# A transposed copy of the input, partial first chunks and a reordered half-step schedule at the head of a two-layer trunk kernel

## The reference, cut to what matters

```python
def rms_norm(x, g):
    y = x * lax.rsqrt(jnp.mean(x * x, axis=-1, keepdims=True) + EPS)
    return y * g
def moba_mixer(h, w_qkv, q_gain, k_gain, w_o, pos):
    q, k, v = jnp.split(h @ w_qkv, 3, axis=-1)
    q = rope(rms_norm(q.reshape(B, S, A_HEADS, A_HEAD_DIM), q_gain), pos)
    k = rope(rms_norm(k.reshape(B, S, A_HEADS, A_HEAD_DIM), k_gain), pos)
    o = moba_attention(...)          # causal softmax(q k^T / sqrt(128)) v
    return o.reshape(B, S, D_MODEL) @ w_o
def reference(...):
    for i in range(DEPTH):
        h = rms_norm(x, norm_mix_g[i])
        x = x + (moba_mixer(h, ...) if i == 0 else retention_mixer(h, ...))
        x = x + sqrelu_mlp(rms_norm(x, norm_mlp_g[i]), mlp_w1[i], mlp_w2[i])
```

## Time and profile before

| | |
|---|---|
| median of 3 runs | 688.73 us (688.31 to 689.94) |
| the profiled execution, its own time | 689.67 us |
| span of its instructions | 687.8 us |
| PE busy | 664.2 us, 97% of the span |
| DVE, ACT, POOL busy | 420.4, 328.6, 27.8 us |
| moved by DMA | 121.93 MB, mean 177 GB/s |

### The profile page before, as it was taken

How to read it: one execution, slowest core, us unless ns; L and a number is a source line. 1 busy time by engine, 2 the same in 40 slices (tenths; PEclk the granted TensorE clock), 3 DMA queues, 4 the chain that set the end, 5 groups by cost and what they waited for, 6 DMA issues and landing times.

```text
span 687.8 us, 8852 instructions
## 1 busy us (share of the span) xinstructions
PE 664.2 (97%) x3293; PEld 558.7 (81%) x3293; DVE 420.4 (61%) x454; ACT 328.6 (48%) x423; POOL 27.8 (4%) x39
## 2 busy tenths in 40 slices
PE   2989899999999999999999999999999999999998
PEld 2868777888888888888888888888888888888886
DVE  2885755677777535446985456555468777743430
ACT  3765655475555433436444554553365555533320
POOL 3032200000000000000000000000000000000000
PEclk9999999999999999999999999999999999999999
DMA  8964344756655555563655554455646665555600
GB/s 286 336 217 149 122 123 123 229 152 204 195 183 183 186 200 203 187 202 124 190 193 180 180 176 130 177 182 154 202 133 199 194 205 195 185 183 186 211 1 30
DMA packets 81469, 121.93 MB, mean 177 GB/s; under 512 B 2032, under 2 KB 43152, under 8 KB 81440
## 3 DMA queue, kind: packets, MB, share of 16 engines
q1 hardware_dynamic: 80736, 119.55, 53.4%
q0 software_dynamic: 496, 1.90, 1.0%
q10 hardware_dynamic: 208, 0.08, 0.1%
HBM read 120.47 MB, written 1.05 MB: 177 GB/s over the span
## 4 chain that ended last, share of the span: by engine, by line
PE 83%; issue 5%; ACT 4%; DVE 4%; DMA 2%; POOL 1%; SPq 0%; DVEq 0%; ACTq 0%; POOLq 0%
PE acc L467 22%; PE acc L427 16%; PE acc L429 16%; PE acc L428 15%; PE acc L470 11%; ACT hi L658 2%; DVE lo L874 2%; DMA x<-in_x 2%; POOL small L383 1%; PE scr L483 1%; ACT probs L726 1%; DVE h_both L883 1%; PE scr L603 1%; POOL rot L403 1%; PE scr L615 1%
## 5 line engine op out<-in xcount | busy, mean ns | idle before, releaser
L874 DVE TENSOR_TENSOR lo<-raw,hi 128x2048 fp32r<-128x2048 f32 x112 | 256.8, 2293 | 141.2 <-ACT hi L658 141.2
L658 ACT ACTIVATE hi<-raw 128x2048 fp32r<-128x2048 f32 x112 | 214.6, 1918 | 127.8 <-PE acc L429 127.8
L467 PE MATMUL acc<-h_both,hi 128*128 128x512 f32 x640 | 223.1, 395 | 0.0
L470 PE MATMUL acc<-h_both,lo 128*128 128x256 f32 x640 | 177.8, 278 | 0.0
L467 PEld LDWEIGHTS acc<-h_both,hi 128*128 128x128 f32 x640 | 120.1, 188 | 28.2
L470 PEld LDWEIGHTS acc<-h_both,lo 128*128 128x128 f32 x640 | 120.3, 188 | 0.0
L427 PE MATMUL acc<-hi,aT_hi 128*128 128x512 f32 x256 | 99.7, 389 | 0.0
L429 PE MATMUL acc<-hi,aT_lo 128*128 128x512 f32 x256 | 99.6, 389 | 0.0
L428 PE MATMUL acc<-lo,aT_hi 128*128 128x512 f32 x256 | 99.6, 389 | 0.0
L427 PE MATMUL acc<-hi,h_both 128*128 128x512 f32 x224 | 91.3, 408 | 0.0
L429 PE MATMUL acc<-hi,h_both 128*128 128x512 f32 x224 | 88.4, 395 | 0.0
(11 more groups left out here) (114 smaller groups left out, 528.5 us busy)
## 6 DMA issues: line engine op xcount, KB each, us to landing
raw<-in_mlp_w SPq DMA_DIRECT2D x64, 1024.0 KB, 5.4
raw<-in_r_w_in SPq DMA_DIRECT2D x24, 1024.0 KB, 5.1
raw<-in_a_w_qkv SPq DMA_DIRECT2D x12, 1024.0 KB, 6.2
raw<-in_r_w_out SPq DMA_DIRECT2D x8, 1024.0 KB, 5.0
raw<-in_a_w_o SPq DMA_DIRECT2D x4, 1024.0 KB, 5.1
x<-in_x SPq DMA_DIRECT2D x2, 512.0 KB, 11.8
out_x<-x SPq DMA_DIRECT2D x4, 256.0 KB, 3.9
decay_sb<-in_decay POOLq DMA_DIRECT2D x1, 768.0 KB, 7.2
```

What stands on the lines that cost most here:

```text
L467: nc.tensor.matmul(bank, feat_view(hi, s)[:, kt, o * P:(o + 1) * P], h_both[:, kt, :, :].rearrange("p b t -> p (b t)"), start=kt == 0, sto ...
L470: m = nc.tensor.matmul(bank[:, 0:SEQ], feat_view(lo, s)[:, kt, o * P:(o + 1) * P], hT_hi[:, kt, :], start=False, stop=kt == KD - 1)
L658: nc.scalar.activation(hi[:, s, :], raw[:, s, :], ACT.Copy).then_inc(hi_ready, 1)
L874: nc.vector.tensor_tensor(lo[:, s, :], raw[:, s, :], hi[:, s, :].bitcast(F32), ALU.subtract).then_inc(lo_ready, 1)
```

## The change

1. **Input.** The host lays out x transposed as well (`xT_src`, two halves of 4 column blocks) and the identity with all norm gains in one array (`consts`). ACT and DVE make `h_both` straight from the loaded `xT_in`. The transposes of the gains and of x in norm 0 are gone. PE does four float32 matmuls on zeros instead, before its first product.
2. **Queues.** All in SP's queue, in this order: first half of xT, chunk 0 in four parts of 256 KB, second half of xT, chunks 1 and 2 in four parts each, `rope_t`, two gains, chunks 3 and 4, x whole (1 MB), chunk 5, `mask`, chunks 6 on. `rope_r_sb` is issued later, beside `decay_sb`. POOL issues nothing at the head.
3. **Parts.** For chunks 0 to 2 ACT and DVE make the high and low part in four pieces of 512 columns, and PE waits for each piece alone. The order on both: xT blocks 0 to 3, chunk 0, xT blocks 4 to 7, chunk 1, chunk 2.
4. **Squares of x.** ACT's squares and the row factor (`square`, `factors`) go to half step 7. var p is not before half step 8. A new step `left` (only the semaphore that frees the accumulator) stays where var was. Each p has its own sums (`head_sums`).
5. **Low parts.** ACT's high part stays at half step k (`high`), DVE's low part goes to k + 1 (`low`), for chunks 3 to 16.

```diff
 def attention_schedule():
     at = [[] for _ in range(SLOTS)]
     for k in range(0, SLOTS, 2):
-        at[k].append(("split", k // 2 + AHEAD))
+        at[k].append(("high", k // 2 + AHEAD))
+        at[k + 1].append(("low", k // 2 + AHEAD))
     for b in range(4):
         for t in range(TT):
             p = 2 * b + t
             at[4 * b + 3 + t] += [("rope", p), ("raw", p)]
-            at[4 * b + 4 + t].append(("var", p))
+            at[4 * b + 4 + t].append(("left", p))
+            at[max(4 * b + 4 + t, FACTORS_AT + 1)].append(("var", p))
...
+    first_to_last = ["O", "N", "v", "rope", "high", "low", "raw", "left", "square", "factors", "var", "T", "A",
+                     "P", "S", "E"]
     for k in range(SLOTS):
...
+FACTORS_AT = 7
...
+SQUARES_BEFORE = sum(what == "raw" for k in range(FACTORS_AT + 1) for what, _ in SCHEDULE[k])
+PARTS = 3
...
-            for n in range(2):
-                sp.dma_start(x[:, :, n * NC:(n + 1) * NC],
-                             xv[:, :, n * NC:(n + 1) * NC]).then_inc(x_in_ready[n], 16)
-            for c in range(1, 12):
+            def load_xT(n):
+                sp.dma_start(xT_in[:, 4 * n:4 * n + 4, :], xT_src[n]).then_inc(xT_in_ready[n], 16)
+
+            def load_parts(c):
+                for kt in range(4):
+                    sp.dma_start(tok_view(raw, c)[:, kt, :],
+                                 qkv_w[QKV_ORDER[c // 2], c % 2][:, kt, :]).then_inc(part_in[c][kt], 16)
+
+            load_xT(0)
+            load_parts(0)
+            load_xT(1)
+            load_parts(1)
+            load_parts(2)
+            sp.dma_start(rope_t[:], rope_a).then_inc(tables_in, 16)
+            for i, g in enumerate((a_q_gain, a_k_gain)):
+                sp.dma_start(gains[:, i, :], g.broadcast_to([P, P])).then_inc(tables_in, 16)
+            load_qkv(3)
+            load_qkv(4)
+            sp.dma_start(x[:], xv).then_inc(x_in_ready, 16)
+            load_qkv(5)
+            sp.dma_start(mask[:], causal).then_inc(mask_in, 16)
...
         def _(pool):
-            pool.dma_start(rope_t[:], rope_a).then_inc(tables_in, 16)
-            for i, g in enumerate((a_q_gain, a_k_gain)):
-                pool.dma_start(gains[:, i, :], g.broadcast_to([P, P])).then_inc(tables_in, 16)
-            pool.dma_start(mask[:], causal).then_inc(tables_in, 16)
-            pool.dma_start(rope_r_sb[:], rope_r).then_inc(tables_r_in, 16)
             half_set = pl.mark(nc.gpsimd.memset(half[:], -0.5))
             pool.wait_ge(pl.sem, half_set)
-            pool.wait_ge(tables_in, 16 * 4)
...
-            norm_power()
             pool.wait_ge(pl.sem, pl.now())
             pool.sem_inc(tables_g_ready, 1)
+            norm_power()
             for p_i in range(8):
...
+            pool.dma_start(rope_r_sb[:], rope_r).then_inc(tables_r_in, 16)
...
-                chunk_in(c_g, s)
+                parts = isinstance(c_g, int) and c_g == 0 and s < PARTS
+                if not parts:
+                    chunk_in(c_g, s)
...
                     for kt in range(4):
                         k = k0 + kt
+                        if parts and t == 0:
+                            if s < 2:
+                                pe.wait_ge(hT_ready, 4 + k + 1)
+                            if kt < 3:
+                                pe.wait_ge(part_lo_ready, 3 * s + kt + 1)
+                            else:
+                                chunk_in(c_g, s)
...
-            pe.wait_ge(ident_in_sem, 16)
-            pe.wait_ge(gains_in, 32)
-            nc.tensor.transpose(acc[:, 0, 0:4 * KD], gain_rows[:],
-                                ident[0:4 * KD, 0:4 * KD]).then_inc(gainsT_ready, 1)
-            for n in range(2):
-                pe.wait_ge(x_in_ready[n], 16)
-                transpose_x(0, range(4 * n, 4 * n + 4))
+            pe.wait_ge(zeros_ready, 1)
+            for _ in range(4):
+                nc.tensor.matmul(acc[:, 3, 0:SEQ], sT[:, 0:P], sT[:, 0:SEQ], start=True, stop=True)
+            pe.wait_ge(consts_in, 16)
...
+                if norm == 0:
+                    act.wait_ge(x_in_ready, 16)
+                    act.wait_ge(squares_qk, 4 * SQUARES_BEFORE)
...
-            act.dma_start(ident[:], ident_in).then_inc(ident_in_sem, 16)
-            for i, g in enumerate((norm_mix_g, norm_mlp_g)):
-                act.dma_start(gain_rows[i * 2 * KD:(i + 1) * 2 * KD, :],
-                              g.rearrange("l (kt p) -> (l kt) p", p=P)).then_inc(gains_in, 16)
-            act.wait_ge(gainsT_ready, 1)
-            nc.scalar.copy(gcol[:].rearrange("p a b -> p (a b)"), acc[:, 0, 0:4 * KD]).then_inc(gcol_ready, 1)
-            split(0, 0)
-            act.wait_ge(gcol_ready, 1)
-            norm_hi(0, range(KD))
-            split(0, 1)
-            norm_squares(0)
-            split(0, 2)
+            def first_hi(kts):
+                for kt in kts:
+                    act.wait_ge(xT_in_ready[kt // 4], 16)
+                    nc.scalar.activation(hT_hi[:, kt, :], xT_in[:, kt, :], ACT.Copy,
+                                         scale=gcol[:, GAIN[0], kt:kt + 1]).then_inc(hT_hi_ready, 1)
+
+            def part_hi(c):
+                for kt in range(4):
+                    act.wait_ge(part_in[c][kt], 16)
+                    nc.scalar.activation(tok_view(hi, c)[:, kt, :], tok_view(raw, c)[:, kt, :], ACT.Copy
+                                         ).then_inc(part_hi_ready if kt < 3 else hi_ready, 1)
+
+            act.dma_start(consts[:], consts_src).then_inc(consts_in, 16)
+            act.wait_ge(consts_in, 16)
+            first_hi(range(4))
+            part_hi(0)
+            first_hi(range(4, KD))
+            part_hi(1)
+            part_hi(2)
...
                 j, t = p_i // 2, p_i % 2
                 act.wait_ge(rope_read, p_i + 1)
-                if p_i == 0:
+                if p_i >= 1:
+                    act.wait_ge(squares_qk, 4 * p_i)
+                if p_i == SQUARES_BEFORE:
                     act.wait_ge(ssq_ready, 4)
-                else:
-                    act.wait_ge(squares_qk, 4 * p_i)
-                if p_i >= 2:
-                    act.wait_ge(pow_ready, p_i)
                 for h in range(4):
                     nc.scalar.activation(junk[:, h * P:(h + 1) * P], acc[:, p_i % 4, h * P:(h + 1) * P],
-                                         ACT.Square, accum_out=small[:, 4 * t + h:4 * t + h + 1]
+                                         ACT.Square, accum_out=head_sums[:, p_i, h:h + 1]
...
+            def first_lo(kts):
+                dve.wait_ge(consts_in, 16)
+                for kt in kts:
+                    dve.wait_ge(hT_hi_ready, kt + 1)
+                    nc.vector.scalar_tensor_tensor(hT_lo[:, kt, :], xT_in[:, kt, :],
+                                                   gcol[:, GAIN[0], kt:kt + 1],
+                                                   hT_hi[:, kt, :].bitcast(F32), ALU.mult,
+                                                   ALU.subtract).then_inc(hT_ready, 1)
+
+            def part_lo(c):
+                for kt in range(4):
+                    if kt < 3:
+                        dve.wait_ge(part_hi_ready, 3 * c + kt + 1)
+                    else:
+                        dve.wait_ge(hi_ready, c + 1)
+                    nc.vector.tensor_tensor(tok_view(lo, c)[:, kt, :], tok_view(raw, c)[:, kt, :],
+                                            tok_view(hi, c)[:, kt, :].bitcast(F32), ALU.subtract
+                                            ).then_inc(part_lo_ready if kt < 3 else lo_ready, 1)
+
+            def first_factors():
+                norm_factors(0)
+                own(nc.vector.tensor_scalar(nrm[:, 5, :], nrm[:, 0, :], EPS, None, ALU.mult))
+                own(nc.vector.tensor_scalar(nrm[:, 6, :], nrm[:, 0, :], EPS * P, None, ALU.mult))
+
+            nc.vector.memset(sT[:], 0.0).then_inc(zeros_ready, 1)
+            first_lo(range(4))
+            part_lo(0)
+            first_lo(range(4, KD))
+            part_lo(1)
+            part_lo(2)
...
                 j, t = p_i // 2, p_i % 2
@@ -928,6 +986,8 @@
                     dve.wait_ge(tok0_ready, j + 1)
                 else:
                     dve.wait_ge(used, 2 * j + 2 + RING)
+                if p_i == 0:
+                    dve.wait_ge(tables_g_ready, 1)
...
                 rr = rot[:, t, :].rearrange("p (h o d) -> p h o d", o=2, d=64)
                 nc.vector.tensor_tensor(rr, rr, ur, ALU.add).then_inc(rot_sum_ready, 1)
+            def head_left(p_i):
+                dve.wait_ge(squares_qk, 4 * p_i + 4)
+                dve.sem_inc(acc_free, 1)
+
             def head_variance(p_i):
                 j, t = p_i // 2, p_i % 2
-                ss = small[:, 4 * t:4 * t + 4]
+                ss = head_sums[:, p_i, :]
                 dve.wait_ge(squares_qk, 4 * p_i + 4)
-                dve.sem_inc(acc_free, 1)
                 if j % 2 == 0:
                     i = nc.vector.tensor_scalar(ss, ss, nrm[:, 6, t:t + 1], None, ALU.add)
```

(23 more changed lines are left out.)

70 lines of the change are left out of this document (35 added, 35 removed).

## The result

| | before | after |
|---|---|---|
| median | 688.55 us (687.75 to 689.94, 6 runs) | 693.0 us (691.32 to 695.07, 6 runs) |
| the profiled execution, its own time | 689.67 us | 693.57 us |
| span of its instructions | 687.8 us | 691.8 us |

The ratio is 1.0059, 95% interval 1.0045 to 1.0073: the change makes the kernel slower by 0.45 to 0.73%. The forecast was 680.9 (677.0 to 685.0), faster. It was off by 12 us, and in the sign.

The account below looks back on a forecast made before the run. PE, busy 97% of the span, was taken as the bound, improvable only in its gaps and slower stretches. Gains of 5.5 (T 2), 1.0 (T 6) and 1.3 (later low parts) sum to 7.8 us: median 680.9, range 677.0 to 685.0.

Parts of the forecast that it names:

- The step that failed: Behind the attention: largest sum of PE's waits for one line is 0.5 us, code left alone, so no gain or loss.
- Rival 4: Slower: gains in the weights' queue delay chunk 3; at 26.3 the 7.8 us are gone, at 30 us 692.4; chance 0.04.
- T 2: PE's transposes of the first k block, opened by DVE and POOL: at 46.5 in place of 52.01, gain 5.5 us.
- The first product: PE's first product in the head: at 7.5 instead of 16.87, 9.4 us earlier.
- Chunk 3: Weights landing in SP's queue: 17.5 without a slow stretch, 19.5 with it, 18.5 taken; ACT's high part then starts the chain.
- the term of 5.7 MB: Bytes loaded up to chunk 3 (xT, chunks 0 to 2, tables, chunk 3), at 0.393 MB per us.
- The POOL term: Before T 2: POOL's powers 1 and 2 and the scaling wait for DVE's low 7, ending at 43.4, and finish at 46.4.
- the 49 that the prediction named as a sign of being wrong: The prediction called itself wrong if T 2 opens before 44 or after 49.
- The clock: Behind the wait at T 2 the clock drops as before: no difference counted, bounds 0 and 1 us more.
- T 6: Later in the attention, PE waits 1.8 us for POOL's scaling: gain between 0 and 1.8, 1.0 taken.
- The later low parts: Low 13 and 14 move behind S 4 and S 6, easing 1.8 us of oT_lo waits: gain 1.3 us taken.
- rival 2: In the attention, later half steps give nothing; only T 2 moves, by 4.4 to 5.5 us: 683.2 to 684.4; chance 0.20.

Follow-up runs that it names:

- experiment 1: The changed kernel with an unused 384-byte tile in front of the arena, back at its old address: 686.56 us, ratio 0.9967 to before.
- experiment 2: The kernel before with gain_rows moved behind the arena and 128 bytes ahead of it, so the arena starts 384 bytes lower: 694.7 us, ratio 1.0095.
- experiment 7: experiment 1 with the two gains laid out for all partitions in memory, no row read 128 times: 684.24 us, ratio 0.9949 to before.
- experiment 10: experiment 1 with ten matmuls on zeros into an unused bank in front of T 2: 684.71 us, ratio 0.9960 to before.
- experiment 11: The changes of experiment 7 and experiment 9 together: 680.89 us, ratio 0.9891 to before.
- experiment 3: The changed kernel with 256 bytes of padding in front of the arena: 694.8 us.
- experiment 4: The changed kernel with weights, h_both and arena all moved, by paddings of 128 bytes in all: 685.27 us.
- experiment 9: experiment 1 with the squares of x and the row factor at half step 5 instead of 7: 683.37 us, ratio 0.9934 to before.
- experiment 5: The changed kernel with 128 bytes of padding in front of the arena: 684.65 us.
- experiment 6: The changed kernel with 448 bytes of padding in front of the arena: 691.87 us.
- experiment 8: experiment 1 with the low parts back in the half step of their high parts: 692.75 us, ratio 1.0076 to before.
- experiment 12: experiment 11 with the low parts from half step 20 on back in the half step of their high parts: 681.54 us, ratio 0.9895.

## Why the prediction was wrong, by its own steps

**The step that failed** is the sentence "Behind the attention the largest sum for one line is 0.5 us, and the change leaves that code alone". The code was left alone, its data were not: two small tiles changed in size, the arena moved by 384 bytes, and about 1,056 products got 5.7 ns longer. The prediction has no term for it. It is +6.0 us by the steps, +5.8 between the marks, +6.4 by experiment 1, +6.5 by experiment 2. With it, the sign of the result is explained: experiment 1 is the change without it, and is 2.0 us faster than before. That was shown both ways, by taking the shift out of after and by putting it into before. None of the four rivals had it. Rival 4, the one on the other side, had the right sign for a wrong reason: chunk 3 came at 20.9, far from the 26.3 at which it decides. That its 692.4 is near the 693.0 measured is luck.

**Experiment 1 against the sum of 7.8 us.** Experiment 1 lies 5.7 us above the forecast even so, and above its range. In the traces T 2 gained 2.4 us there in place of 5.5, and what was to gain 2.3 more behind T 2 gained nothing.

- *The first product*, forecast 7.5, came at 9.07. The sum had no term for ACT's table load of 1.28 us in front of the first block. PE waited 3.5 us for the first piece of chunk 0, and came to T 2 at 43.4, not at 39.9. As the forecast said, it made no difference to T 2.
- *Chunk 3*, forecast 18.5 between bounds of 17.5 and 19.5, was split from 20.94 on, beyond the slow bound. The reading that the gains cause the slow stretch was right (experiment 7), and so was its price: 2.2 us by the windows, 2.0 in the sum. ACT was not late, it stood idle 5.41 us for the load. What was too small is the term of 5.7 MB: added up from the windows, 6.4 MB had been moved when chunk 3's high part could start in after, and 6.3 MB at 18.85 in experiment 7. The 0.6 to 0.7 MB more can only be bytes of loads issued behind chunk 3, and at 0.393 MB per us they are 1.6 us. So chunk 3 without the stretch comes at 18.85, not at 17.5.
- *T 2*, forecast 46.5 (45.5 to 47.6), came at 48.77. The 2.3 us are chunk 3's 2.4. From chunk 3's high part to T 2 it was 28.0 us forecast and 27.8 measured: the order on DVE, the stand for the row factor (forecast "2 to 3 us", found 1.29 and 0.81), and the power held behind low 7 all stood as worked out. The POOL term, "43.4 + 0.9 + 1.0 + 1.05", was 45.76 to 48.72, 2.96 against 2.95. This term gave 3.2 in place of 5.5. In experiment 1, with chunk 3 at 21.69, T 2 is at 49.59, behind the 49 that the prediction named as a sign of being wrong.
- *The clock*, counted as no difference with a bound of 1. Its lower level lasted 6.8 us. The traces price it by the stretch from T 2 to x in kernels with the new schedule: 71.4 and 71.5 us without the lower level (experiments 10 and 11), 73.0 to 73.1 with 3.4 us of it (3, 4, 9), 73.4 to 74.3 with 6.8 (after, 1, 5, 6, 7). So the second 3.4 us, which before doesn't have, cost 0.3 to 1.3 us, 0.9 in the mean, near the forecast's bound.
- *T 6*, forecast a gain of 1.0: 1.8 of waits became 0.8 (6.2 less 5.4). Right.
- *The later low parts*, forecast 1.3: they gained nothing. In place of 1.8 us for `oT_lo` and 0.2 for `v_att` PE waits 1.0 and 1.8, 0.8 more. Low 14 now stands in front of the mask of head 7 on DVE, the exponential of head 7 and then the copy of V stand behind it on ACT, and the product of the first head with that V is late. It is what rival 2 said, "a low part in front of another step holds that one in turn", and it took back most of the gain at T 6. Experiments 8 and 12, which undo it, have the old waits again.

So without the arena the chain of rival 2 was the nearest (683.2 to 684.4), with chunk 3 later than the slow bound. Experiment 7 ends at 684.2, inside that rival's range, but it is another kernel and the kernel before was 1.4 us faster beside it; that agreement is no evidence.

**What was right**: that T 2 bounds the head and not the products; that 9.4 us at the first product would shrink there; which of the steps in front of T 2 is last; that PE waits longer there than before.

**What stays open.** The products with `h_both` as the moving operand (640 with 512 columns and 640 with 256 in turn, in three stages: the first matrix of each MLP, and q and k of the retention) go at one of two paces in each stage. Their 512-column steps come at 231.4 to 232.2 ns or at 235.7 to 237.0, with their addresses as they were in all kernels but experiment 4, which moves both operands alike. No stage is slow in experiments 2, 4, 5, 6, 10 and 11; one is in before (q and k), after (the first MLP), 1, 7, 8 and 12; two are in 3 and 9. Together they take from 221.2 to 224.6 us, so two profiled executions can differ by 3.4 us for this alone. Its cause wasn't tried, and since each kernel has one trace, no run shows whether the same kernel changes from execution to execution; the times of experiment 9 (681.97 to 686.19) would leave room for it. Whether the spread read makes the slow stretch of before too, in POOL's queue, was not tried. Nor was the reason for the 256 bytes tried: that the loading of a stationary operand meets the running product's reads in the same part of SBUF fits the rows, but no run shows it.

## What to carry to other kernels

When a diff adds or removes a tile, write down the start of every later operand of a large product modulo 256 bytes, before and after; if two operands of a product fall apart, put a padding in. When a change is to end one engine's first wait, follow the fixed order to the next point where all engines meet, and price the change there; here 7.8 us at the first product were 3.2 at T 2. A part that gains and a part that loses can lie far apart: mark both traces at a few points they have in common (here the updates of x) before explaining anything. When two profiled executions are compared, measure first how far like kernels differ at the same point (here 1.5 us at T 2, 3.4 in the products with `h_both` moving), and explain only what is larger than that.

## What the runs showed of the hardware

- **A product's step depends on where its two operands start.** With 512 columns of float32 in the fp32r form: 226.7 ns when the stationary and the moving operand start at the same place modulo 256 bytes of a partition, 232.4 at a distance of 128, 233.3 at 64. Other distances weren't run. In this kernel, with the products over the arena alone, that was 6 us of 690. The Trainium skill, "TensorE: Matmul & The Clock Gate", "Step-by-step: what each phase is for", says that loading the next weights doesn't take SBUF read bandwidth from the running matmul. It states nothing on where they start. Here the place makes 5.7 ns a product; whether the two reads are what meets, no run shows.
- **A row read 128 times slows the whole traffic.** Two gains of 64 KB each, spread from one row of 512 bytes, took the core's traffic from 371 GB/s to 136, 109 and 171 in the three us that followed, with the DMA engines' busy share down at 0.55; laid out, it was 362 at the least. The windows of before (137 GB/s from 7 to 10, with the gains in POOL's queue) look alike, but their share is 1.02, and no experiment took the gains out there.
- **A wait can leave the clock low for longer than it lasts, and not by its length alone.** At T 2 the granted clock was at its lower level for 3.4 us around waits of 3.0 and 3.8 us, for 6.8 around 4.0 and 5.4, for 10.2 around 10.4. Around waits of 4.9 us it was for 3.4 once (experiment 4) and for 6.8 three times (1, 5, 6), around 2.1 for 3.4 twice (9, 12) and not at all once (11), and around 2.6 not at all (2).
